# Where the split operands of TensorE start in SBUF: slots of weights 16 bytes further apart, MLP operands 64 bytes later in odd layers

## The reference

```python
for i in range(4):                      # mixers: MLA, MoBA, SSD, MLA
    x = x + mixer_i(rmsnorm(x, norm_mix[i]))
    h = rmsnorm(x, norm_mlp[i])
    x = x + square(relu(h @ w1[i])) @ w2[i]     # w1: 1024 x 4096, w2: 4096 x 1024
return rmsnorm(x, norm_final)
```

## Time and profile before

| what | value |
|---|---|
| median of three executions | 1312.21 us (1311.41 to 1316.04) |
| profiled execution: span from first to last instruction | 1312.0 us |
| TensorE busy | 1286.5 us (98%), 7578 matmuls |
| VectorE, ScalarE busy | 891.4 us (68%), 671.6 us (51%) |
| granted TensorE clock, mean | 0.998 of full speed |
| HBM traffic | 227.08 MB read, 175 GB/s |

### The profile page before, as it was taken

How to read it: one execution, slowest core, us unless ns; L and a number is a source line. 1 busy time by engine, 2 the same in 40 slices (tenths; PEclk the granted TensorE clock), 3 DMA queues, 4 the chain that set the end, 5 groups by cost and what they waited for, 6 DMA issues and landing times.

```text
span 1312.0 us, 18369 instructions
## 1 busy us (share of the span) xinstructions
PE 1286.5 (98%) x7578; PEld 1126.3 (86%) x7578; DVE 891.4 (68%) x1180; ACT 671.6 (51%) x861; POOL 43.5 (3%) x58
## 2 busy tenths in 40 slices
PE   6999999999999999999999999999999999999998
PEld 5888888888999888887999888888887888888886
DVE  5877666665666666666899886766667876666664
ACT  5555554444555454444776644544445645454442
POOL 3000000000000000000101110000000000000000
PEclk9999999999999999999999999999999999999999
DMA  9744465555845475545574643755554334565540
GB/s 289 143 168 148 141 232 201 193 192 161 233 149 180 132 254 192 192 165 160 181 222 141 203 149 119 249 191 192 191 180 140 117 130 130 168 231 193 192 161 32
DMA packets 146067, 230.93 MB, mean 176 GB/s; under 512 B 7683, under 2 KB 112429, under 8 KB 145984
## 3 DMA queue, kind: packets, MB, share of 16 engines
q1 hardware_dynamic: 143136, 221.66, 50.8%
q0 software_dynamic: 2848, 8.10, 2.9%
HBM read 227.08 MB, written 2.65 MB: 175 GB/s over the span
## 4 chain that ended last, share of the span: by engine, by line
PE 88%; DVE 7%; DMA 1%; issue 1%; ACT 1%; POOL 1%; SPq 0%; POOLq 0%; DVEq 0%; ACTq 0%
PE bank L982 15%; PE acc L902 12%; PE acc L903 12%; PE acc L906 12%; PE bank L987 8%; PE bank L590 7%; PE bank L591 7%; PE bank L592 7%; DVE wlo L573 2%; PE bank L1402 1%; PE bank L1105 1%; PE bank L795 1%; PE bank L1408 1%; PE bank L1090 1%; DMA raw<-in_mla_w_in 1%
## 5 line engine op out<-in xcount | busy, mean ns | idle before, releaser
L573 DVE TENSOR_TENSOR wlo<-raw,whi 128x2048 fp32r<-128x2048 f32 (+2 forms) x207 | 464.7, 2255 | 139.6 <-ACT whi L557 139.5
L557 ACT ACTIVATE whi<-raw 128x2048 fp32r<-128x2048 f32 (+2 forms) x207 | 386.8, 1879 | 45.8 <-PE acc L906 44.2
L982 PE MATMUL bank<-hsplit,whi 128*128 128x512 f32 x896 | 212.2, 389 | 0.0
L903 PE MATMUL acc<-wlo,uhi 128*128 128x512 f32 x512 | 200.1, 391 | 0.0
L902 PE MATMUL acc<-whi,uhi 128*128 128x512 f32 x512 | 199.6, 390 | 0.0
L982 PEld LDWEIGHTS bank<-hsplit,whi 128*128 128x128 f32 x896 | 168.2, 188 | 34.9
L906 PE MATMUL acc<-whi,ulo 128*128 128x512 f32 x512 | 159.2, 390 | 0.0
L590 PE MATMUL bank<-hsplit,whi 128*128 128x256 f32 (+2 forms) x540 | 154.5, 286 | 0.3 <-DVE xn L1980 0.3
L592 PE MATMUL bank<-hsplit,wlo 128*128 128x256 f32 (+2 forms) x540 | 151.4, 280 | 0.0
L591 PE MATMUL bank<-hsplit,whi 128*128 128x256 f32 (+2 forms) x540 | 151.4, 280 | 0.0
L1027 ACT ACTIVATE relu<-bank 128x512 f32<-128x512 f32 x56 | 33.5, 598 | 188.9 <-PE bank L987 188.9
(11 more groups left out here) (252 smaller groups left out, 1813.4 us busy)
## 6 DMA issues: line engine op xcount, KB each, us to landing
raw<-in_mlp_w SPq DMA_DIRECT2D x128, 1024.0 KB, 5.5
raw<-in_ssd_w_in SPq DMA_DIRECT2D x18, 1024.0 KB, 5.4
raw<-in_mla_w_o SPq DMA_DIRECT2D x16, 1024.0 KB, 4.9
raw<-in_mla_w_ukv SPq DMA_DIRECT2D x8, 1024.0 KB, 5.8
raw<-in_moba_w_qkv SPq DMA_DIRECT2D x16, 512.0 KB, 5.3
raw<-in_ssd_w_out SPq DMA_DIRECT2D x8, 1024.0 KB, 4.9
raw<-in_mla_w_uq SPq DMA_DIRECT2D x8, 768.0 KB, 6.0
raw<-in_mla_w_in SPq DMA_DIRECT2D x4, 1024.0 KB, 7.5
```

What stands on the lines that cost most here:

```text
L557: nc.scalar.activation(whi[:, s, lo:e], raw[:, s, lo:e], ACT.Copy).then_inc(w_hi_done[s], 1)
L573: nc.vector.tensor_tensor(wlo[:, s, lo:e], raw[:, s, lo:e], whi[:, s, lo:e].bitcast(F32), ALU.subtract).then_inc(w_split[s], 1)
L903: nc.tensor.matmul(acc[t][half][:], lh, wl[:, k, n], start=False, stop=False)
L982: nc.tensor.matmul(ps, w[0][:, k, m * P:(m + 1) * P], hflat[:, k].rearrange("p a n -> p (a n)"), start=k == 0, stop=False)
```

## The change

Each slot of `whi` and `wlo` gets 4 more floats behind it, so slot s starts 16·s bytes later than before. `hflat`, `uhi` and `ulo` become lists by layer, and in layers 1 and 3 the data start 16 floats (64 bytes) later; for this the rows of `uhi` and `ulo` are 32 floats longer. In the built program two more things follow: `whi` as a whole has grown by 64 bytes, so `wlo` starts 64 bytes later, and all behind `wlo`, the input among it, 128 bytes later than before.

```diff
+SKEW = 4
...
-        whi = sb("whi", [P, SLOTS, UNIT], F32R)
-        wlo = sb("wlo", [P, SLOTS, UNIT], F32R)
+        whi_rows = sb("whi", [P, SLOTS * (UNIT + SKEW)], F32R)
+        wlo_rows = sb("wlo", [P, SLOTS * (UNIT + SKEW)], F32R)
+        whi = [whi_rows[:, (UNIT + SKEW) * s:(UNIT + SKEW) * s + UNIT] for s in range(SLOTS)]
+        wlo = [wlo_rows[:, (UNIT + SKEW) * s:(UNIT + SKEW) * s + UNIT] for s in range(SLOTS)]
...
-        hflat = hrows[:].rearrange("p k n -> p (k n)")[:, 0:KD * 2 * SEQ].rearrange("p (k a n) -> p k a n", k=KD, a=2)
+
+        def shift(L):
+            return 16 * (L % 2)
+
+        hflat = [hrows[:].rearrange("p k n -> p (k n)")[:, shift(L):shift(L) + KD * 2 * SEQ].rearrange(
+            "p (k a n) -> p k a n", k=KD, a=2) for L in range(DEPTH)]
...
-            uhi = sb("uhi", [P, 2, 2, SEQ], F32R, stage)
-            ulo = sb("ulo", [P, 2, 2, SEQ], F32R, stage)
+            u_rows = [sb(n, [P, 2, 2 * SEQ + 32], F32R, stage) for n in ("uhi", "ulo")]
+            uhi, ulo = ([u[:, :, shift(L):shift(L) + 2 * SEQ].rearrange("p b (a n) -> p b a n", a=2) for L in range(DEPTH)]
+                        for u in u_rows)
...
-            return (whi[:, s, off:off + a * b].rearrange("p (a b) -> p a b", a=a),
-                    wlo[:, s, off:off + a * b].rearrange("p (a b) -> p a b", a=a))
+            return (whi[s][:, off:off + a * b].rearrange("p (a b) -> p a b", a=a),
+                    wlo[s][:, off:off + a * b].rearrange("p (a b) -> p a b", a=a))
...
-                    nc.tensor.matmul(ps, w[0][:, k, m * P:(m + 1) * P], hflat[:, k].rearrange("p a n -> p (a n)"),
+                    nc.tensor.matmul(ps, w[0][:, k, m * P:(m + 1) * P], hflat[L][:, k].rearrange("p a n -> p (a n)"),
...
-                return uhi[:, c % 2], ulo[:, c % 2]
+                return uhi[L][:, c % 2], ulo[L][:, c % 2]
```

More of the change, by code:

```diff
@@ L555, in act_splits @@
                     lo = e // 2
-                    nc.scalar.activation(whi[:, s, :lo], raw[:, s, :lo], ACT.Copy).then_inc(half_hi_done, 1)
-                nc.scalar.activation(whi[:, s, lo:e], raw[:, s, lo:e], ACT.Copy).then_inc(w_hi_done[s], 1)
+                    nc.scalar.activation(whi[s][:, :lo], raw[:, s, :lo], ACT.Copy).then_inc(half_hi_done, 1)
+                nc.scalar.activation(whi[s][:, lo:e], raw[:, s, lo:e], ACT.Copy).then_inc(w_hi_done[s], 1)
                 split_to["act"] += 1
@@ L569, in dve_splits @@
                     dve.wait_ge(half_hi_done, n + 1)
-                    nc.vector.tensor_tensor(wlo[:, s, :lo], raw[:, s, :lo], whi[:, s, :lo].bitcast(F32),
+                    nc.vector.tensor_tensor(wlo[s][:, :lo], raw[:, s, :lo], whi[s][:, :lo].bitcast(F32),
                                             ALU.subtract).then_inc(half_split, 1)
                 dve.wait_ge(w_hi_done[s], k + 1)
-                nc.vector.tensor_tensor(wlo[:, s, lo:e], raw[:, s, lo:e], whi[:, s, lo:e].bitcast(F32),
+                nc.vector.tensor_tensor(wlo[s][:, lo:e], raw[:, s, lo:e], whi[s][:, lo:e].bitcast(F32),
                                         ALU.subtract).then_inc(w_split[s], 1)
@@ L637, in split_input @@
         def split_input(j):
-            h = hflat if deferred(j) else hsplit
+            h = hflat[stages[j][1]] if deferred(j) else hsplit
             return h[:, :, 0, :], h[:, :, 1, :]
@@ L986, in pe_up @@
                 for k in range(KD):
-                    mm = nc.tensor.matmul(ps[:, 0:SEQ], w[1][:, k, m * P:(m + 1) * P], hflat[:, k, 0, :], start=False,
+                    mm = nc.tensor.matmul(ps[:, 0:SEQ], w[1][:, k, m * P:(m + 1) * P], hflat[L][:, k, 0, :], start=False,
                                           stop=k == KD - 1)
@@ L1031, in act_mlp @@
                     act.wait_ge(*used(("down", L, c - 2)))
-                nc.scalar.activation(uhi[:, c % 2].rearrange("p a b -> p (a b)"), rsq[:, c % 2, :],
+                nc.scalar.activation(uhi[L][:, c % 2].rearrange("p a b -> p (a b)"), rsq[:, c % 2, :],
                                      ACT.Copy).then_inc(uhi_done, 1)
@@ L1052, in dve_mlp @@
                 dve.wait_ge(uhi_done, n + 1)
-                nc.vector.tensor_tensor(ulo[:, c % 2].rearrange("p a b -> p (a b)"), rsq[:, c % 2, :],
-                                        uhi[:, c % 2].rearrange("p a b -> p (a b)").bitcast(F32),
+                nc.vector.tensor_tensor(ulo[L][:, c % 2].rearrange("p a b -> p (a b)"), rsq[:, c % 2, :],
+                                        uhi[L][:, c % 2].rearrange("p a b -> p (a b)").bitcast(F32),
                                         ALU.subtract).then_inc(ulo_done, 1)
```

## The result

The changed kernel takes 1327.74 us (median of four executions, 1325.33 to 1330.96), the kernel before, run beside it, 1313.50 us (four, 1311.41 to 1316.04): a ratio of 1.0103, 95% interval 1.0084 to 1.0122. The profiled execution took 1325.33 us, its span 1323.5 us, 11.5 more than the 1312.0 of before; it was the fastest of the four and had the highest mean granted clock (0.999, the others 0.996).

The account below looks back on a forecast made before the run. TensorE was taken as the bound: nearly the number of matmuls by the distance between starts. +14.0 - 4.3 + 1.0 = +10.7 us on a span of 1312.0 gave 1322.7, about 1323 us; 8-in-10 range 1297 to 1332.

Parts of the forecast that it names:

- slower by the long matmuls: The forecast case: 512-column matmuls lose time on leaving offset 0; about 1323 us, own range 1317 to 1332, chance 0.42.
- The 0.2 us added for the step from span to device time: Whole kernel: the median was taken to stand 0.2 us above the span, turning 1322.7 into about 1323 us.
- Long matmuls, +14.0 us: 512-column matmuls leaving offset 0 modulo 128: 2800 at +5 ns each, +14.0 us, bounds -17.9 to +18.8.
- one in eight stays there, 2800 leave: Of 3200 long matmuls at offset 0, spread evenly over eight offsets, one in eight keeps offset 0 and 2800 leave.
- The step that I trusted least: Long matmuls: the +5 ns price, taken from offset 64 alone, was carried over to all seven new offsets.
- Short matmuls at offset 0, -4.3 us: 256-column matmuls: 1530 of 1750 leave offset 0, going from 120.0 to about 117.2 ns, -4.3 us.
- Short matmuls at offset 64, +1.0 us: 1460 short matmuls: one in eight comes to offset 0, +0.5 us; 180 mostly lose their best state, +0.5 us.
- The splits, nothing: ScalarE's and VectorE's splits on rows starting 16, 32 or 48 bytes later: costed at nothing.
- No effect: Rival: offsets within 64 bytes alike, or long matmuls lose only about 1.5 ns; 1313 us, chance 0.25.
- Faster: Rival: half the new offsets let long matmuls escape a steady collision, -6.4 ns each; -12.3 us, 1300 us, chance 0.28.
- Slower through the splits: Rival: addresses off 64-byte multiples slow VectorE's split, 9 us more in the mixers; 1332 us, chance 0.05.
- What the trace was to show: Chain: 16 long pieces 3.63 to 3.70-3.74 us, short 1.91 to 1.87 or below; long records 393 ns or more; split 2255.

Follow-up runs that it names:

- the pads of 128 and 256 bytes: Kernel before with 128 or 256 unused bytes behind `wlo`, moving all tiles behind it: 1327.62 us (ratio 1.0090) and 1314.16 us (1.0000).
- the kernel with the places alone: Kernel before plus 64 unused bytes behind `whi` and 64 behind `wlo`, without slot gaps or later odd layers: 1328.71 us, ratio 1.0105.
- the pad of 192 bytes: Kernel before with 192 unused bytes behind `wlo`, so all tiles behind it lie later: 1319.07 us, ratio 1.0036.
- a common shift of 64 bytes: Kernel before with 64 unused bytes ahead of `raw`, so every tile lies 64 bytes later: 1315.28 us, ratio 1.0016.
- the pads of 16 to 192 bytes: Kernel before with unused bytes behind `wlo`: 16 (32 as built) 1330.21 us, 64 1330.36, 128 1327.62, 192 1319.07.
- the version with the low parts moved: Kernel before with only the low parts of the MLPs' first weights 64 bytes beyond their moving operand modulo 256, `kp` moved: 1313.92 us, ratio 1.0000.

## Why the prediction was right, and where it was not

**The time.** 1323 was forecast, 1327.74 measured, the case "slower by the long matmuls" as it said, inside its own range of 1317 to 1332. The change itself was forecast at +10.7 us and measured at +14.2 by the medians taken side by side. The 0.2 us added for the step from span to device time was no constant: in every execution of these runs the device time stands 1.7 to 1.9 us above its own span.

**Long matmuls, +14.0 us.** The price was +5 ns from one row at offset 64; measured is +4.4 (227.8 to 232.2). Times 3200 that is +14.2 us. The size is right, but not the count, "one in eight stays there, 2800 leave". I counted offsets modulo 128, by which slot 0 of an even layer lies as before. The change moves everything behind `wlo` by 128 bytes, and modulo 256, as the pads of 128 and 256 bytes show, that is a departure too: L991 from slot 0 in layer 2, at an offset of 0 and a distance of 128, has 232.3 ns in the changed kernel. All 3200 left; a price 0.6 ns too high and a count 400 too low cancelled, which is luck. More than the count hangs on it: by offsets modulo 128 the kernel with the places alone would have lost nothing, and it lost as much as the whole change. The step that I trusted least, one offset carried over to seven, held: by distance the long matmuls of the changed kernel have means of 229.6 to 233.4 ns, and none of them is back at 227.

**Short matmuls at offset 0, -4.3 us.** The term was too large. They went from 119.6 to 118.3 ns, 1.3 and not 2.8 less, -2.3 us by the 1716 of them in the trace.

**Short matmuls at offset 64, +1.0 us.** Measured 116.8 to 117.9 ns, 1445 of them: +1.6 us. Together with the term before -0.7 where -3.3 was forecast. Averaged over the eight offsets the good and bad states of short matmuls simply mix.

**The splits, nothing.** 2255 ns before and after, and TensorE waits no longer for them. The rest of the span, 11.5 - 14.2 + 0.7 = -2.0 us, I had not forecast. Most of it is the granted clock of the kernel before. In a window at the start of layer 2 its profiled execution has this (start and end us, length, TensorE busy us, matmuls, mean granted clock, DMA share, GB/s):

```profile
617.00:629.00 12.00, 8.91 (x52) 0.86 0.11 40
```

The 0.86 is 3.4 us at half clock, from 624.3 to 627.7 us, behind two waits of TensorE of 2.4 and 0.7 us. The changed kernel has the same waits and stays at full clock there, and the same matmuls take 1.6 us less. So the 11.5 us between the two profiled spans understate the loss.

**The rivals.** *No effect* needed +1.5 ns per long matmul and got +4.4. *Faster* needed long matmuls that come out on average below +1.2 ns. With the pad of 192 bytes they come out at +2.6, with those of 32, 64 and 128 at +4.7 to +5.4. Only one large group escapes, and by 0.8 ns, not 6.4: the 512 of L904 in the kernel with 192 bytes. *Slower through the splits* fell with the 2255 ns. The reasoning for the faster rival, that the equal start is a steady collision and leaving it can help, is turned round by the records: with equal starts the long matmuls of the up products run at one even spacing of 226.7 ns, and every other distance tried breaks that up. What they then pay is not constant (records of 387 to 404 ns in the changed kernel).

**What the trace was to show.** Right for the long pieces: 3.70 to 3.74 us "in most chunks" came out as 49 of 56 at 3.71 to 3.74, different by slot (229.7 and 233.9 ns for the two slots of layer 0), and mean records of 393 or more as 394 and 395. Not right for the short pieces: 1.87 or below is reached by 8 of 56.

**Read ports.** With not one instruction changed, 128 unused bytes cost 13 us, all of it in the spacing of long matmuls whose stationary and moving operand start at different distances from a multiple of 256 bytes. The Trainium skill, "TensorE: Matmul & The Clock Gate" (Step-by-step: what each phase is for), has the two operands come through independent read ports; by that rule, as the prediction drew on it, no distance between the two could matter, and the runs decide against that, for float32 operands of this kind and this size. Whether it is the ports that interfere they do not show.

**What is shown and what is not.** Shown: the loss comes with the distance between the operands of long matmuls, 256 bytes count as none, a common shift of 64 bytes does nothing, and the loss is there while VectorE and ScalarE stand idle. Not shown: which stationary operand counts, a matmul's own or the next one's, since in nearly all pairs here the two start alike modulo 256. Not shown: why. That loading the next stationary operand and reading the moving one disturb each other is my reading of it; no run here took one of the two reads away. Nor is shown why 192 bytes cost less than 32, 64 and 128.

## What to carry to other kernels

Where TensorE is the bound, compare the spacing of the same matmuls at different addresses, and look up the start addresses in the built program after every edit of a tile, since a pad or a longer row moves all tiles declared behind it. For split float32 operands with 512 columns, keep the stationary and the moving one at the same start modulo 256 bytes, rows and slots included; leaving it by a pad of 32 to 192 bytes cost 0.4% to 1.1% here. Look at the granted clock of each execution before calling a difference of 1 or 2 us real or absent. Take the price of an address from a run, not from another place in the kernel: the same distance gave short matmuls 113.7 ns in one kernel and 117.7 in another.

## What the runs showed of the hardware that was not expected

- **A step of 226.7 ns.** With equal starts modulo 256, the long matmuls of L982 within a chunk stand 226 or 227 ns apart, 840 of 840 pairs; with the pads of 16 to 192 bytes the means of the two large kinds, up and down, lie between 229.0 and 233.4 ns.
- **The sign.** With the moving operand starting 64 bytes above the stationary one, long matmuls took 231.4 and 229.0 ns in the kernels with 64 and 192 bytes of pad; 64 bytes below it (192), 233.4 in both; but 229.8 with the places alone.
- **Neighbours matter.** Long matmuls with equal starts had 232.9 instead of 229.4 ns over the ten that follow short ones, when only the low parts that the short ones load were moved, by 192 bytes; moved by 64 they had 229.6. Short matmuls whose moving operand starts 64 bytes below the stationary one: 113.7 ns after long ones of the same distance (the kernel with 192 bytes), 117.7 after long ones with equal starts (the version with the low parts moved). That the matmuls before the short ones set this is the one difference I see between the two, and was not tested by itself.
- **At half clock the extra is gone.** In the 3.4 us at half clock (1.2 GHz), which the part on the splits tells of, ten matmuls of 256 columns stand 213 or 214 ns apart, which is one column a cycle and nothing besides; the same ten in the changed kernel, at full clock, stand 113 to 121 ns apart, where one column a cycle would be 106.7.
